# Two transformer blocks on one core: the order of four steps, and where the roots of the half norms are kept

## What is computed

```
def first_block(x, c, ...):
    cos, sin = _rope_tables(L)
    c_act = jax.nn.silu(c)
    for l in range(DEPTH):
        mod = c_act @ w_mod[l] + b_mod[l]
        sh1, sc1, g1, sh2, sc2, g2 = [m[:, None, :] for m in jnp.split(mod, 6, axis=-1)]
        h = _rms(x, ln1[l]) * (1 + sc1) + sh1
        x = x + g1 * _mixing(h, w_in[l], ...)
        h = _rms(x, ln2[l]) * (1 + sc2) + sh2
        x = x + g2 * _swiglu(h, w_gate[l], w_up[l], w_down[l])
    return x

def second_block(x, c, positions, ...):
    cos, sin = _rope_tables_2(positions)
    cond = jax.nn.silu(c)
    for l in range(DEPTH):
        mod = (cond @ w_ada[l] + b_ada[l])[:, None, :]
        sh_m, sc_m, g_m, sh_f, sc_f, g_f = jnp.split(mod, 6, axis=-1)
        h = _rmsnorm(x, norm_g[l, 0]) * (1.0 + sc_m) + sh_m
        y = _hybrid_mixer(h, cos, sin, l, w_in[l], ...)
        x = x + g_m * _rmsnorm(y, norm_g[l, 1])
        h = _rmsnorm(x, norm_g[l, 2]) * (1.0 + sc_f) + sh_f
        y = _sq_relu_mlp(h, w_up[l], w_down[l])
        x = x + g_f * _rmsnorm(y, norm_g[l, 3])
    return x
```

## Time and profile before

| | |
|---|---|
| median of three runs | 3231.54 us (3217.03 to 3239.86) |
| the profiled execution | 3235.96 us, span 3234.2 us |
| granted clock of TensorE, mean | 0.952 |
| PE busy | 3009.4 us, 93% |
| DVE busy | 1803.9 us, 56% |
| POOL busy | 931.8 us, 29% |
| ACT busy | 773.2 us, 24% |

### The profile page before, as it was taken

One profiled execution on the slowest core, in us unless ns is written; L12 is line 12 of the kernel. 1 busy time (PEld: TensorE's weight loads), 2 busy tenths in 40 slices (PEclk: granted clock), 3 DMA queues, 4 the chain that ended last, 5 costly groups with the idle time before them and its releaser, 6 DMA issues.

```text
span 3234.2 us, 34034 instructions
## 1 busy us (share of the span) xinstructions
PE 3009.4 (93%) x12282; PEld 2164.4 (67%) x12282; DVE 1803.9 (56%) x3823; ACT 773.2 (24%) x1801; POOL 931.8 (29%) x802
## 2 busy tenths in 40 slices
PE   7988999999899799999989998899998998899997
PEld 3445578888644567888754355788884345688886
DVE  1484359568438646947952634787924444551333
ACT  2244320000124442000022244210112235420111
POOL 0220124443312013444420301344440210243442
PEclk9997899999999799999989989999999998899998
DMA  5105125335211002434421101154421110122221
GB/s 219 71 27 183 52 87 184 107 131 179 105 52 53 27 27 91 172 128 143 147 88 55 52 27 61 65 200 158 169 105 48 35 52 27 53 79 81 101 79 53
DMA packets 39223, 304.93 MB, mean 94 GB/s; under 512 B 4352, under 2 KB 4480, under 8 KB 24848
## 3 DMA queue, kind: packets, MB, share of 16 engines
q1 hardware_dynamic: 39024, 302.68, 25.9%
q0 software_dynamic: 32, 0.07, 0.0%
HBM read 300.63 MB, written 2.10 MB: 94 GB/s over the span
## 4 chain that ended last, share of the span: by engine, by line
PE 71%; DVE 16%; ACT 5%; issue 3%; DMA 3%; POOL 1%; DVEq 0%; SPq 0%; ACTq 0%; POOLq 0%
PE bank L1077 37%; PE bank L1057 9%; PE bank L1405 7%; PE bank L1131 3%; PE bank L1223 3%; DVE nw L2033 3%; DMA ring<-in_slabs 2%; DVE sel L2272 1%; DVE m L2271 1%; PE bank L1538 1%; PE bank L1273 1%; DVE SPT L2336 1%; ACT SPT L1725 1%; PE bank L1260 1%; PE bank L1188 1%
## 5 line engine op out<-in xcount | busy, mean ns | idle before, releaser
L962 POOL TENSOR_TENSOR SPT<-ring 128x512 f32<-128x512 f32 (+2 forms) x140 | 175.6, 1254 | 964.7 <-DMA ring<-in_slabs 503.4
L1077 PE MATMUL bank<-U,ring 128*128 128x256 f32 x1728 | 409.6, 382 | 12.6 <-DVE U L2067 10.7
L1077 PEld LDWEIGHTS bank<-U,ring 128*128 128x128 f32 x1728 | 330.3, 191 | 60.2 <-DVE U L2067 12.3
L2033 DVE SCALAR_TENSOR_TENSOR nw<-sel,c,nw 128x256 f32<-128x256 f32 x504 | 329.5, 654 | 37.6 <-DMA sel<-in_mod_pieces 19.9
L1077 PE MATMUL bank<-U,SPT 128*128 128x256 f32 x1296 | 313.1, 381 | 5.3 <-POOL SPT L967 5.3
L1077 PEld LDWEIGHTS bank<-U,SPT 128*128 128x128 f32 x1296 | 247.4, 191 | 40.9 <-POOL SPT L967 6.9
L1405 PE MATMUL bank<-hT,ring 128*128 128x512 f32 x544 | 252.6, 609 | 6.8 <-ACT hT L1842 6.8
L1077 PE MATMUL bank<-hT,SPT 128*128 128x256 f32 x1088 | 257.0, 379 | 0.0
L1223 PE MATMUL bank<-hT,ring 128*128 128x512 f32 x512 | 242.8, 617 | 4.7 <-ACT hT L1621 4.7
L1077 PE MATMUL bank<-hT,ring 128*128 128x256 f32 x1088 | 246.0, 379 | 0.0
L2093 DVE TENSOR_TENSOR rb<-bank,nw 128x256 f32<-128x256 f32 x108 | 45.6, 422 | 354.2 <-PE bank L1077 257.4
(11 more groups left out here) (343 smaller groups left out, 4658.7 us busy)
## 6 DMA issues: line engine op xcount, KB each, us to landing
ring<-in_slabs SPq DMA_DIRECT2D x88, 2048.0 KB, 8.3
sel<-in_mod_pieces SPq DMA_DIRECT2D x144, 512.0 KB, 4.7
ring<-in_slabs SPq DMA_DIRECT2D x8, 1536.0 KB, 6.7
ring<-in_slabs SPq DMA_DIRECT2D x8, 1280.0 KB, 8.9
ring<-in_slabs SPq DMA_DIRECT2D x2, 2080.0 KB, 8.5
ring<-in_slabs SPq DMA_DIRECT2D x2, 1808.0 KB, 9.2
ring<-in_slabs SPq DMA_DIRECT2D x2, 1664.0 KB, 7.6
cst<-in_consts SPq DMA_DIRECT2D x1, 2112.0 KB, 14.6
```

The lines of the kernel that those rows point to most:

```text
L962: pool.tensor_tensor(e1, a21, a22, ALU.add).then_inc(*pool_order.up())
L1077: mm = pe.matmul(into[j][:, c:c + HALF], lhs[:, k, :], rhs[:, k, :], start=(begin and k == 0), stop=(end and k == kp - 1))
L2033: ins = dve.scalar_tensor_tensor(a, w[:, k, :], c[:, j:j + 1], a, ALU.mult, ALU.add)
```

## The change

It has four parts of order and one of place.

1. In `ffn_steps`, `turn` stands right behind its unit and `S`, ahead of `ma`, `ma` and `mt` of the same step, and `mm` and `mb` come one unit later.
2. In `order1` the six `idx` steps stand in the tiles 5, 6 and 7, two in each, behind the second and the fourth part of the tile.
3. `angles` is split in three, at units 13, 15 and 17 of the last MLP of block 1, and the sine becomes a step `sine` at unit 19. Its scratch moves to `yB`, and the explicit load of tables behind it is gone.
4. `ns` of both halves (both blocks) and `post` of both halves (block 2) have fixed banks. The root (Exp) is written into the bank that held the sum, DVE's multiplies read it there, and DVE frees the bank when all eight are done. Of `ns` the whole-sequence form stays as it was.

The diff, cut to what is used below:

```diff
+HALF_BANKS = {("post", 0, 0): (4,), ("post", 0, 1): (5,), ("ns", 1, 0): (7,), ("ns", 1, 1): (6,)}
...
+ANGLES_AT = {13: [("angles", 0)], 15: [("angles", 1)], 17: [("angles", 2)], 19: [("sine",)]}
...
-        if when and t == when[-1] + 2:
+        if when and t == when[-1] + 3:
             o.append(("mb", at))
...
+        if u[0] == "gu" and u[2] == wide - 1:
+            o.append(("turn", u[1]))
         if t in when:
             p = when.index(t)
             o += [("ma", 2 * p), ("ma", 2 * p + 1), ("mt", p)]
-        if when and t == when[-1] + 1:
+        if when and t == when[-1] + 2:
             at = 4 * ((turn + 1) % 2)
             o.append(("mm", at))
-        if u[0] == "gu" and u[2] == wide - 1:
-            o.append(("turn", u[1]))
         o += after(t)
...
-        o += [st for part in tile(m) for st in part]
+        for q, part in enumerate(tile(m)):
+            o += part + ([("idx", m - 4, q // 2)] if m >= 5 and q % 2 else [])
...
+                def root_kept(job, r, done):
+
+                    act.wait_ge(*bk2.ready(l, job))
+                    b, c = bank[bk2.bank(l, job)], SIDES[job[2]]
+                    act.activation(rb[:, r, c], b[:, c], ACT.Ln, bias=eps, scale=1.0 / D).then_inc(*act_order.up())
+                    act.wait_ge(*act_order.last())
+                    act.activation(b[:, c], rb[:, r, c], ACT.Exp, scale=-0.5).then_inc(*done)
...
-                            dve.tensor_tensor(hT[:, k, c], xT[:, k, c], rb[:, 0, c], ALU.mult).then_inc(
+                            dve.tensor_tensor(hT[:, k, c], xT[:, k, c], src[:, c] if w else rb[:, 0, c], ALU.mult).then_inc(
                                 *s2["xn"].up())
+                        if w:
+                            dve.wait_ge(*s2["xn"].now())
+                            dve.sem_inc(*freed)
...
-                        link(dve.scalar_tensor_tensor(y, y, modG[:, 0, k:k + 1], rb[:, 0, c], ALU.mult, ALU.mult))
+                        b = bk2.bank(l, ("post", 0, s))
+                        link(dve.scalar_tensor_tensor(y, y, modG[:, 0, k:k + 1], bank[b][:, c], ALU.mult, ALU.mult))
+                        if k == KT - 1:
+                            dve.sem_inc(free[b], 1)
```

More of the change, by code:

```diff
@@ L355, in order1 @@
             o.append(("tables",))
-        o += [st for part in tile(m) for st in part]
+        for q, part in enumerate(tile(m)):
+            o += part + ([("idx", m - 4, q // 2)] if m >= 5 and q % 2 else [])
         if m == 3:
             o += [("projv", i) for i in range(QT)]
-        if m == 5:
-            o += [("idx", i, hp) for i in range(1, QT) for hp in range(2)]
         if m >= 6:
@@ L461, in jobs1 @@
     if kind == "ns":
-        return [(st, SIDE[1:3] if st[1:] == (1, 1) else SIDE)]
+        return [(st, HALF_BANKS.get(st, SIDE))]
     if kind == "mm":
@@ L1600, in _ @@
                         act.wait_ge(*bk1.ready(l, st))
-                        act.activation(rb[:, 0, c], src[:, c], ACT.Ln, bias=eps, scale=1.0 / D).then_inc(*freed)
-                        act.wait_ge(*bk1.taken(l, st))
-                        act.activation(rb[:, 0, c], rb[:, 0, c], ACT.Exp, scale=-0.5).then_inc(*s1["rstd"].up())
+                        if st[1]:
+                            act.activation(rb[:, 0, c], src[:, c], ACT.Ln, bias=eps, scale=1.0 / D).then_inc(*act_order.up())
+                            act.wait_ge(*act_order.last())
+                            act.activation(src[:, c], rb[:, 0, c], ACT.Exp, scale=-0.5).then_inc(*s1["rstd"].up())
+                        else:
+                            act.activation(rb[:, 0, c], src[:, c], ACT.Ln, bias=eps, scale=1.0 / D).then_inc(*freed)
+                            act.wait_ge(*bk1.taken(l, st))
+                            act.activation(rb[:, 0, c], rb[:, 0, c], ACT.Exp, scale=-0.5).then_inc(*s1["rstd"].up())
                     elif kind == "nq":
@@ L1780, in _ @@
                         act.activation(hT[:, k, :], xT[:, k, :], ACT.Square).then_inc(*s1["xs"].up())
-                    elif kind == "angles":
+                    elif kind == "sine":
                         act.wait_ge(pos_ready, 1)
                         act.activation(tab[64:96, :, :], tab[64:96, :, :], ACT.Sin).then_inc(pos_ready, 1)
-                        act.preload_act_table_set("natural_log_exp_and_others")
             for l in range(DEPTH):
@@ L1804, in squares, with root @@
                     act.activation(sqb[:, q % 2, c], src, ACT.Square).then_inc(*s2["psq"].up())
-                def root(job, r, scale, e, done, c=slice(0, SEQ)):
+                def root(job, r, scale, e, done):
                     act.wait_ge(*bk2.ready(l, job))
                     b = bk2.bank(l, job)
-                    act.activation(rb[:, r, c], bank[b][:, c], ACT.Ln, bias=e, scale=scale).then_inc(free[b], 1)
+                    act.activation(rb[:, r, :], bank[b][:, :], ACT.Ln, bias=e, scale=scale).then_inc(free[b], 1)
                     act.wait_ge(*bk2.taken(l, job))
-                    act.activation(rb[:, r, c], rb[:, r, c], ACT.Exp, scale=-0.5).then_inc(*done)
+                    act.activation(rb[:, r, :], rb[:, r, :], ACT.Exp, scale=-0.5).then_inc(*done)
+                def root_kept(job, r, done):
+                    act.wait_ge(*bk2.ready(l, job))
+                    b, c = bank[bk2.bank(l, job)], SIDES[job[2]]
+                    act.activation(rb[:, r, c], b[:, c], ACT.Ln, bias=eps, scale=1.0 / D).then_inc(*act_order.up())
+                    act.wait_ge(*act_order.last())
+                    act.activation(b[:, c], rb[:, r, c], ACT.Exp, scale=-0.5).then_inc(*done)
                 for st in STEPS2[l]:
@@ L1833, in _ @@
                     elif kind == "ns":
-                        root(st, 0, 1.0 / D, eps, s2["rstd"].up(), SIDES[st[2]] if st[1] else slice(0, SEQ))
+                        if st[1]:
+                            root_kept(st, 0, s2["rstd"].up())
+                        else:
+                            root(st, 0, 1.0 / D, eps, s2["rstd"].up())
                     elif kind == "nh":
@@ L2179, in _ @@
                     elif kind == "angles":
-                        dve.wait_ge(pos_in, 16)
                         rows = slice(64, 96)
-                        pf, turns, ang = sqb[rows, 0, :], sqb[rows, 1, :], yB[rows, 0, :]
-                        link(dve.tensor_copy(pf, posi[rows, :]))
-                        link(dve.tensor_scalar(ang, pf, cst[rows, C_MISC + 4:C_MISC + 5], None, ALU.mult))
-                        for t, quarter in ((0, 0.25), (1, 0.0)):
+                        pf, turns, ang = [yB[rows, j, :] for j in range(3)]
+                        if st[1] == 0:
+                            dve.wait_ge(pos_in, 16)
+                            link(dve.tensor_copy(pf, posi[rows, :]))
+                            link(dve.tensor_scalar(ang, pf, cst[rows, C_MISC + 4:C_MISC + 5], None, ALU.mult))
+                        else:
+                            t, quarter = ((0, 0.25), (1, 0.0))[st[1] - 1]
                             a = tab[rows, t, :]
@@ L2225, in _ @@
                         for k in ORDER[w]:
-                            dve.tensor_tensor(hT[:, k, c], xT[:, k, c], rb[:, 0, c], ALU.mult).then_inc(
+                            dve.tensor_tensor(hT[:, k, c], xT[:, k, c], src[:, c] if w else rb[:, 0, c], ALU.mult).then_inc(
                                 *s1["xn"].up())
+                        if w:
+                            dve.wait_ge(*s1["xn"].now())
+                            dve.sem_inc(*freed)
                     elif kind == "pss":
```

15 lines of the change are left out of this document (10 added, 5 removed).

## The result

| kernel | median, us | ratio to before | 95% interval |
|---|---|---|---|
| before, same chips | 3233.72 (3217.03 to 3239.86) | | |
| changed | 3240.35 | 1.0025 | 1.0016 to 1.0034 |

The forecast was 3224, 7.5 us faster. The measured time lies inside the range but on the other side of no change: some 7 us slower. The ratio leaves out one of the 22 executions of the changed kernel, which took 4490 us at a granted clock of 0.643 where the others had 0.954 to 0.959. The profiled execution of the changed kernel has a span of 3237.3 us, 3.1 above that of before.

The account below looks back on a forecast made before the run. PE, with 71% of the chain that ended last (DVE 16%), was taken as the bound. Terms 7 + 15 - 15 - 10.3 - 4.2 = -7.5 from 3231.54 gave 3224 us, range 3194 to 3256.

Parts of the forecast that it names:

- The turn: MLPs of block 1 (both layers) and block 2 (layer 0): turn ahead of the modulation sums, +7 and +15 us.
- 4 x 0.42 = 1.7 us: Price of the four DVE subtractions of a turn that now stand before the sums, 0.42 us each.
- a rival at 0.07: Turns meet POOL's sums: subtractions cost 4.8 us instead of 1.7, 2.9 at each of nine loads; 3268 us, chance 0.07.
- a delay is passed to the load after next: Block 1 MLPs: weight loads alternate in slack, so four and a half of about nine add 1.7 us, 7.7 a layer.
- Block 2's share: Block 2's MLP, layer 0: turns wait 1.82 us for ACT with sums still to do; +15 us, bounds +7 and +22.
- mm, 0 forecast: Folded modulation product one unit later: its 5.9 us waits go, but the slab behind comes no earlier; 0, bound -5.9.
- Half norms: Block 2: first-half multiplies fall from 10.71 to 2.77 us, gain 7.5 a layer, -15 us; block 1: 0.
- PE then has no 26 products left to do: Block 2 half norms: squares are summed as they come, so the second sum ends at 2033.2 instead of 2040.7.
- that case as a bound: Block 2 half norms: if PE's clock stays low after the stall, some 1.4 us a layer of gain is left.
- Index scores: Block 1, both layers: scores spread over tiles 5 to 7 end PE's waits for ACT; 5.1 a layer, -10.3 us.
- Angles: End of block 1, layer 1: PE's wait after the MLP, with the ACT sine, goes; -4.2 us, bounds -2 and -6.
- two rivals beside it: Late slabs hidden, all four turn waits gained: 3191 us, chance 0.16; turns meet POOL: 3268 us, chance 0.07.

Follow-up runs that it names:

- turn_behind: The changed kernel with the turn put back behind the modulation sums (mm stays one unit later): 3201.72 us, ratio 0.9908 to before.

## Why the prediction was wrong, step by step

**The turn, the step that failed: +22 forecast, 38 to 39 measured.** The mechanism was right: turn, sums, SP's slab, POOL, PE, with no slack. Three things in the term were wrong.

The first is the price, "4 x 0.42 = 1.7 us". 0.42 is the row of an operation beside which POOL is idle. The turn stands where a hidden tile closes, and there POOL is summing: 5.6 us for the four, 1.37 each, as the earlier trace rows had shown for a like operation (1.21), and as the second subtraction of the very turn in the earlier trace rows showed:

```profile
2066.20 1.38 DVE L2065 TENSOR_TENSOR U<-U 128x256 f32<-128x256 f32 x1
```

The same prediction used to value the half norms, and gave it to the turns only in a rival at 0.07. Over the 11 turns of a first MLP the mean of one subtraction went from 0.48 to 1.16 us; over all 54 turns from 0.66 to 1.00.

The second is the count, "a delay is passed to the load after next". With the turn alone ahead, PE waits 2.39, 2.38, 2.38 and 1.26 us for POOL at successive loads of layer 0, 26.8, 26.8 and 25.7 us apart: each of the four is late, not every second one, though by less than the 3.8 that the sums are; in layer 1 it is three of the first four. Waits on slabs and their sums rose by 11.8 us in layer 0 and 10.7 in layer 1, forecast 7.7 each; the waits for the turned tile that went were 4.9 and 5.9, forecast 4.2.

The third is a term put at nothing without a reason: products that run slower behind the stops, which the prediction thought of only at the half norms. PE's idle time in the three MLPs grew by 24.9 us, close to the 22, and the same products took 13.0 longer. Layer 0's granted clock fell from 0.995 to 0.979. That the idle time alone comes near 22 is luck, made of a low price and too few loads against more time gained at the turned tile and a block 2 forecast too high (next paragraph). Undoing the turn gives a like split: between changed and turn_behind PE's idle time in the three MLPs differs by 20.9 us, the products by 8.8. How much the products lose varies between executions: layer 0's took 386 to 390 us in the six profiles with the turn ahead and late slabs, and 382 and 386 in before and turn_behind.

The rival's price, 2.9 a load, was nearer than the forecast's 1.7; its nine loads at that price, 22 a layer, were too many.

**Block 2's share, +15 forecast, +17.9 measured.** Each turn waits 1.82 for ACT, and the slabs are late by more from one to the next. PE's waits on slabs in the earlier trace rows's MLP rose in the first half from 2.7 to 9.1 us and in the second, for which I took 4, from 0 to 5.9: about 12 where 15 was forecast. Products that took 5 us longer (382.8 for 377.8) make up nearly all of the rest, so that the closeness of the two numbers is in part luck.

**mm, 0 forecast.** Right in size, +1.3 by the medians of the experiment. The reason given is borne out in part: of the 3.2 us of waits at the mm that the move takes away, 1.0 is back on slabs and their sums. It is no property of mm: once slabs are early, its listed wait is 8.2 us with the old place.

**Half norms, -15 forecast, -11.7 in the traces, 9.5 by undoing it.** The multiplies took 2.73 (forecast 2.77), the bank's release let PE start 3.16 us after them (forecast 3.0), the adds ended 13.1 us after the first multiply (forecast 13.0). What failed is "PE then has no 26 products left to do": the 32 first products took 9.86 us at a granted clock of 0.72, so the sums of squares came as a block of 16 behind them, 3.62 us, and not as the squares came. The prediction named that case as a bound, at 1.4 a layer; it came out between the two, near 6. The 62 cycles that the Trainium skill's table has more for a PSUM source than for SBUF (VectorE: DVE Perf Modes, the section on the TRN2 errata), by estimate 65 ns at its 0.96 GHz, don't show in this form, with one operand in a bank and one in SBUF: the eight multiplies with a bank took 2.73 us, where eight with both operands in SBUF, and POOL idle, take 2.77.

**Index scores, -10.3 forecast, about -4 in traces of like clock and -12.9 by the medians.** The step at the place itself held: at the first output product behind the projections of layer 1 the changed kernel has gained 4.5 against the stage's start (forecast 5.1). By the MLP 3.2 of it are given back, in the later part of the mixing, where the same products run at a lower clock (before first, then changed):

```profile
1102.70:1199.00 96.30, 88.41 (x401) 57.55 (x400) 44.49 (x121) 42.02 (x102) 13.23 (x28) 0.91 0.00 1
```

```profile
1093.30:1193.00 99.70, 92.48 (x401) 59.09 (x400) 44.00 (x121) 41.94 (x101) 13.25 (x28) 0.87 0.00 1
```

401 products in both, 96.3 us before and 99.7 changed, with DVE, ACT and POOL as busy as each other. Why the clock is lower there isn't settled by these runs. Nor is it settled that spreading the scores keeps the clock in layer 0 up: none of eight profiles with the scores spread had the slower layer 0 and two of four with them together did, which points that way with few executions. The forecast had no such term; if it holds, the -12.9 of the medians comes near the -10.3 partly by luck.

**Angles, -4.2 forecast, 6.0 by undoing.** Right in kind; behind the wait two products took 2.04 us instead of 1.02, which adds to it.

**The sum.** Without the turn the prediction's parts make -29.5; the kernel without it (turn_behind) measured 30 below before by the ratio and 32 to 33 by the medians. That is in part luck: in its profile layer 0 of the mixing gains 14.5 us, where 5.1 was forecast, and the half norms and layer 1 less than forecast. The forecast fell on the wrong side because of one term, +22 for 38. All the signs that the prediction named came true (fast multiplies, no wait at the scores, turns that wait 1.8, more waits on slabs); none of them tests the size of that term. The likeliest case was given 0.68, and two rivals beside it, on this one term, 0.16 and 0.07 on its two sides. The measured time is inside the range, since that was drawn from both.

## What to carry to other kernels

Price a moved operation by the neighbours it will have at its new place, not at its old one: subtractions with two operands in SBUF took 1.37 us beside GpSimd's sums and 0.42 without, and the turn stands just where those sums run. Add to the price of new stops what the products behind them lose; here that was a third of the whole. When a transfer's queue holds small pieces that wait for an engine's work, with the large ones that the bound engine needs behind them, look there before ordering that engine's work; one line in the queue's order was worth 77 us together with the turn order that alone cost 39, 16.5 with the turn behind, and about 5, not clear of noise, on the kernel before. And a wait on the list tells little of its price: with the queue as it was, the 10.7 us for the turned tile couldn't be had, as the next wait stood right behind; with the queue changed the same waits were listed at 20.2 and worth 21.9.

## What the runs showed of the hardware

- A subtraction of VectorE with two SBUF operands (128 x 256) took 1.37 to 1.38 us beside GpSimd's sums and 0.42 otherwise; eight multiplies with one operand in a bank took 2.73 us beside GpSimd's sums and 2.74 without. The Trainium skill has the rule (SBUF — State Buffer, "Who interferes with whom": an instruction of VectorE with two SBUF inputs contends with one of GpSimd that reads SBUF, one with at most one SBUF input and outside the 2-port perf modes does not); the traces agree with it for these two. A TENSOR_SCALAR (L2050), which reads one SBUF tile, took 1.35 us beside the sums at 1314.85 and 0.35 at 1323.64, where GpSimd was idle: one tile in SBUF is not safe in every form.
- A stop of TensorE of 2 to 5 us can cost more than itself: after one of 2.38 us the granted clock was 0.57 for four microseconds, and eight products took 3.62 us instead of 1.99. Of 20 stops of 1.5 to 5.2 us at the MLP products of the changed kernel, nine had eight products of 2.69 to 3.78 us behind them and eleven had 1.99, some of these after stops of the same 2.38 (at 564.2, for one).
- Executions with the same steps differ by where the clock is low: a stretch of block 1, layer 0, ran at 0.73 in two profiles and at 0.84 in two others, worth 11 to 12 us over the stage, which is more than most parts of this change.
